# A hybrid decoder layer: one bank per part of the sample bias table, later stores of the states, and other places for three loads in sample attention

## The reference, cut to what matters

```
z = rmsnorm(x) @ w_in                      # 7 groups of 512 columns: retention q,k,v,gate; attention q,k,v
retention: o = (q k^T * decay) v + q S     # 8 heads of 64; samples start from the given state S
           S_new = S * g^C + k^T v         # state_ret_sample is an output: (8, 8, 64, 64)
attention: p = softmax(q k^T + bias[distance]);  o = p v
           # samples see a cache of 2048 keys per sequence through the dilated patterns
mix = [retention, attention] @ w_out;  x = x + rmsnorm(mix);  x = x + rmsnorm(swiglu(x))
```

## Time and profile before

| | us |
|---|---|
| median of 3 runs (1657.44 to 1664.04) | 1659.31 |
| the profiled execution | 1659.42 |
| its span, first to last instruction | 1657.9 |
| TensorE busy, share of the span | 1553.1 (94%) |
| VectorE / ScalarE / GpSimd busy | 614.4 / 410.9 / 384.4 |
| mean granted TensorE clock | 0.977 of full |
| retention ends / prompt attention ends / sample attention ends | 447 / 606 / 725.7 |

### The profile page before, as it was taken

How to read it: one execution, slowest core, us unless ns; L and a number is a source line. 1 busy time by engine, 2 the same in 40 slices (tenths; PEclk the granted TensorE clock), 3 DMA queues, 4 the chain that set the end, 5 groups by cost and what they waited for, 6 DMA issues and landing times.

```text
span 1657.9 us, 23040 instructions
## 1 busy us (share of the span) xinstructions
PE 1553.1 (94%) x9294; PEld 1345.7 (81%) x9294; DVE 614.4 (37%) x985; ACT 410.9 (25%) x728; POOL 384.4 (23%) x459
## 2 busy tenths in 40 slices
PE   7999999989888878979999999999999999999994
PEld 6788888878555556758899999999999999999983
DVE  2334110107766644524542323232323333333364
ACT  4410122112145533523432121111112111111121
POOL 3255300014322222004562121121212121111111
PEclk9999999989899999979999999999999999999997
DMA  5423434128444039923446543545535365453445
GB/s 201 126 77 127 133 127 163 47 100 293 138 140 153 14 141 412 414 84 115 124 127 191 141 148 106 169 126 152 153 113 159 108 154 138 129 159 107 132 119 165
DMA packets 120290, 245.59 MB, mean 148 GB/s; under 512 B 20652, under 2 KB 82364, under 8 KB 115045
## 3 DMA queue, kind: packets, MB, share of 16 engines
q1 hardware_dynamic: 111400, 157.15, 30.1%
q0 software_dynamic: 6976, 71.32, 14.5%
q10 hardware_dynamic: 1824, 15.83, 2.3%
HBM read 214.08 MB, written 106.21 MB: 193 GB/s over the span
## 4 chain that ended last, share of the span: by engine, by line
PE 47%; POOL 3%; issue 2%; DVE 2%; DMA 1%; ACT 0%; POOLq 0%; ACTq 0%; DVEq 0%
PE y_ps L2181 31%; PE x_ps L2195 8%; PE m_ps L2195 4%; PE d_ps L2195 4%; POOL xm L1655 1%; POOL h_lo L1667 1%; PE y_ps L1785 1%; DMA own<-x_mid_scratch 1%; DVE y L1750 1%; DVE acc L2112 0%; DVE acc L2116 0%; POOL stat L1648 0%; POOL stat L1657 0%; POOL stat L1991 0%; DVE acc L2100 0%
## 5 line engine op out<-in xcount | busy, mean ns | idle before, releaser
L2181 PE MATMUL y_ps<-h_hi,gu_hi 128*128 128x384 f32 (+1 forms) x1056 | 346.1, 328 | 0.0
L2181 PE MATMUL y_ps<-h_hi,gu_lo 128*128 128x384 f32 (+1 forms) x1056 | 345.8, 327 | 0.0
L2181 PE MATMUL y_ps<-h_lo,gu_hi 128*128 128x384 f32 (+1 forms) x1056 | 345.7, 327 | 0.0
L1959 POOL TENSOR_TENSOR f<-silu,f 128x384 fp32r<-128x384 f32 (+1 forms) x66 | 60.4, 915 | 605.0 <-ACT f L2021 417.6
L2181 PEld LDWEIGHTS y_ps<-h_hi,gu_hi 128*128 128x128 f32 x1056 | 198.4, 188 | 2.0
L2181 PEld LDWEIGHTS y_ps<-h_lo,gu_hi 128*128 128x128 f32 x1056 | 198.4, 188 | 1.9
L2181 PEld LDWEIGHTS y_ps<-h_hi,gu_lo 128*128 128x128 f32 x1056 | 198.4, 188 | 0.0
L508 PE MATMUL z_ps<-w_hi,h_hi 128*128 128x512 f32 x488 | 190.7, 391 | 4.3 <-POOL h_lo L336 4.3
L508 PE MATMUL z_ps<-w_lo,h_hi 128*128 128x512 f32 x488 | 190.0, 389 | 0.0
L2092 DVE TENSOR_TENSOR silu<-silu,y_ps 128x384 f32<-128x384 f32 (+1 forms) x66 | 35.1, 532 | 361.2 <-ACT silu L2018 355.5
L508 PE MATMUL z_ps<-w_hi,h_lo 128*128 128x512 f32 x432 | 168.2, 389 | 0.0
(11 more groups left out here) (251 smaller groups left out, 2218.3 us busy)
## 6 DMA issues: line engine op xcount, KB each, us to landing
ks_sample<-cache_k_win POOLq DMA_DIRECT2D x60, 544.0 KB, 6.5
vs_sample<-cache_v_win POOLq DMA_DIRECT2D x60, 544.0 KB, 7.8
raw<-w_gu SPq DMA_DIRECT2D x84, 256.0 KB, 6.6
K<-cache_k_win SPq DMA_DIRECT2D x8, 2048.0 KB
w_raw<-w_in SPq DMA_DIRECT2D x14, 1024.0 KB
z_scratch<-z_out SPq DMA_DIRECT2D x56, 256.0 KB, 2.0
raw<-w_down SPq DMA_DIRECT2D x22, 512.0 KB, 5.7
zr<-z_scratch SPq DMA_DIRECT2D x8, 1024.0 KB, 11.0
```

The lines of the kernel that those rows point to most:

```text
L1959: low = pool.tensor_tensor(f_lo[cut], f_t[:, 0:n_p], f_hi[cut].bitcast(F32), ALU.subtract)
L2181: mm = pe.matmul(bank[u % 2][:, 0:n], w[s][:, k, h, :], x[:, k, c:c + n], start=(k, m) == (0, 0), stop=(k, m) == (KT - 1, 2))
```

## The change

The table's three parts go to three PSUM banks: `table_ps` and the two banks of `qk_ps`. The products of parts 1 and 2 no longer wait for a copy (they wait once for `qkT_ready`, the last copy out of `qk_ps`), and their copies run on ScalarE behind its last square. The two stores of the sample states leave retention's SP program and stand in prompt attention's, after the values of pairs 0 and 1 and ahead of the sample keys; `sout_ready` and `S_out` are handed over. In sample attention `EARLY_KEYS` is 7 in place of 6, the rows and turned rows of output tiles 0 and 1 are loaded behind keys 7, and their x rows behind the second half of the weights.

```diff
-    def build_samples(self, dve, n):
-        dve.wait_ge(self.bias_done, n + 1)
+    def build_samples(self, eng, copy, n, bank):
+        eng.wait_ge(self.bias_done, n + 1)
         w = min(512, self.KEYS - 512 * n)
-        dve.tensor_copy(self.bias_s[:, 512 * n:512 * n + w], self.ps[:, 0:w]).then_inc(self.bias_ready, 1)
+        copy(self.bias_s[:, 512 * n:512 * n + w], bank[:, 0:w]).then_inc(self.bias_ready, 1)
...
-    def sample_products(self, pe, n):
+    def sample_products(self, pe, n, bank):
...
-        else:
-            pe.wait_ge(self.bias_ready, n)
...
-            mm = pe.matmul(self.ps[:, 0:w], self.rel_t[0:k, g].rearrange("n p c r t -> n (p c r t)"),
+            mm = pe.matmul(bank[:, 0:w], self.rel_t[0:k, g].rearrange("n p c r t -> n (p c r t)"),
...
+        table_ps = (tables.ps, *(bank.rearrange("c p n -> c (p n)") for bank in qk_ps))
...
                 store(SAMPLE)
-                sp.wait_ge(sout_ready, 8)
-                for par in range(2):
-                    sp.dma_start(state_s.rearrange("b (p r) d e -> r d b p e", r=2)[par],
-                                 S_out[HD * par:HD * par + HD]).then_inc(state_stored, 16)
                 tables.finish(sp)
...
                 square(SAMPLE)
+                for n in (1, 2):
+                    tables.build_samples(act, act.copy, n, table_ps[n])
...
-                tables.build_samples(dve, 0)
+                tables.build_samples(dve, dve.tensor_copy, 0, table_ps[0])
...
                 decode_state(3)
-                for n in (1, 2):
-                    tables.build_samples(dve, n)
...
-                tables.sample_products(pe, 0)
+                tables.sample_products(pe, 0, table_ps[0])
...
+                pe.wait_ge(qkT_ready, TT)
                 for n in (1, 2):
-                    tables.sample_products(pe, n)
+                    tables.sample_products(pe, n, table_ps[n])
...
                 load_values(0)
                 load_values(1)
+                sp.wait_ge(sout_ready, 2 * NPAIR)
+                for par in range(2):
+                    sp.dma_start(state_s.rearrange("b (p r) d e -> r d b p e", r=2)[par],
+                                 S_out[HD * par:HD * par + HD]).then_inc(retained[2], 16)
                 ahead(sp)
...
-    RING, GROUPS, EARLY_KEYS = 4, 3, 6
+    RING, GROUPS, EARLY_KEYS = 4, 3, 7
...
                 for b in range(2, DEC_B):
-                    if b in (4, 5):
-                        out.load_rows(sp, b - 4)
-                        out.load_turned(sp, b - 4)
-                        out.load_x(sp, b - 4)
                     sp.wait_ge(T_done, key_at(b - 2, STILES - 1) + 1)
                     load_keys(sp, A, z, K, K_landed, b)
+                for t in range(2):
+                    out.load_rows(sp, t)
+                    out.load_turned(sp, t)
                 sp.wait_ge(T_done, key_at(DEC_B - 2, STILES - 1) + 1)
                 out.load_weights(sp, 1, w_b)
+                for t in range(2):
+                    out.load_x(sp, t)
```

More of the change, by code:

```diff
@@ L618, in sample_products, with retention @@
             pe.wait_ge(self.rel_t_ready, 6)
-        else:
-            pe.wait_ge(self.bias_ready, n)
         for g in range(3):
             k = self.rows(g)
-            mm = pe.matmul(self.ps[:, 0:w], self.rel_t[0:k, g].rearrange("n p c r t -> n (p c r t)"),
+            mm = pe.matmul(bank[:, 0:w], self.rel_t[0:k, g].rearrange("n p c r t -> n (p c r t)"),
                            self.dist_s[0:k, g, 512 * n:512 * n + w], start=(g == 0), stop=(g == 2))
         mm.then_inc(self.bias_done, 1)
-def retention(nc, A, z, mix, ident, ret, state_p, state_s, tab, bias_p, bias_s, kept_on, stored, ahead):
+def retention(nc, A, z, mix, ident, ret, state_p, tab, bias_p, bias_s, kept_on, stored, sout_ready, ahead):
     with ExitStack() as ctx:
@@ L655, in retention @@
          mean_ready, oc_ready, sq_ready, square_sum_ready, var_ready, rstd_ready, on_ready, mix_ready, cleared, qd_ready,
-         kd_ready, vm_ready, sout_ready) = map(
+         kd_ready, vm_ready) = map(
             sem, ("state_landed", "qk_turned", "qkT_ready", "inner_done", "inT_ready", "update_done", "S_ready", "last_ready",
                   "o_done", "sum_ready", "mean_ready", "oc_ready", "sq_ready", "square_sum_ready", "var_ready", "rstd_ready",
-                  "on_ready", "mix_ready", "cleared", "qd_ready", "kd_ready", "vm_ready", "sout_ready"))
+                  "on_ready", "mix_ready", "cleared", "qd_ready", "kd_ready", "vm_ready"))
         *mix_stored, state_stored = stored
@@ L968, in __call__, with prompt_attention @@
         return self.nc.alloc_sbuf_tensor_at(name, shape, dtype, offset=here)
-def prompt_attention(nc, A, z, mix_t, bias, ident, q_n, k_n, qk_landed, clear, ahead, second_keys, spare, retained):
+def prompt_attention(nc, A, z, mix_t, bias, ident, q_n, k_n, qk_landed, clear, ahead, second_keys, spare, retained, state_s, S_out, sout_ready):
     UNITS, LAST = NPAIR * PT, NPAIR * PT - 1
@@ L2280, in hymba_layer @@
                                                              ("S_last", [128, NPAIR, HD]))]
+        sout_ready = nc.alloc_semaphore("sout_ready")
         retained = [nc.alloc_semaphore(n) for n in ("mix_stored0", "mix_stored1", "state_stored")]
-        retention(nc, A, z, mix, ident, ret, A["state_p"][0, 0], A["state_s"][0], tab, bias_p, bias_s, kept_on, retained,
+        retention(nc, A, z, mix, ident, ret, A["state_p"][0, 0], tab, bias_p, bias_s, kept_on, retained, sout_ready,
                   lambda sp: load_pair(sp, z, q_n, k_n, qk_landed, 0))
@@ L2300, in hymba_layer @@
                          lambda sp: load_keys(sp, A, z, K, K_landed, 1),
-                         Region(nc, spare_from, spare_to), retained)
+                         Region(nc, spare_from, spare_to), retained, A["state_s"][0], kept_on[1], sout_ready)
         with_2_3.close()
```

## The result

The changed kernel takes 1649.94 us, the median of 7 executions (1647.18 to 1654.17), against 1664.04 for the kernel before in the same comparison (7 executions, 1657.44 to 1667.54). The ratio is 0.9919 with an interval of 0.9903 to 0.9935: faster by some 13.5 us. The profiled execution took 1647.18, its span is 1645.6, and its mean granted clock is 0.981. Against the profiled execution of before (1659.42) that is 12.2 us. The difference of the medians is 14.1.

A forecast was written before the change was run, and what follows sets the result against it. It saw a one-bank ping-pong ending retention, then a clock fall, and a wait for keys in sample attention. Terms 5.6 + 3.6 + 6.0 + 1.0 = 16.2 us, off 1659.4, gave 1643.2 (1637 to 1652).

The forecast's parts named there:

- the clock's fall (1646.8): Rival at the retention boundary: a 2.0 us TensorE wait still lowers the clock, losing 3.6 us; chance 0.25.
- transfers (1647.7): Rival in sample attention: transfers bound it, moved loads give 2.5 us and a seventh tile none; chance 0.17.
- both (1651.3): Rival combining the clock's fall at the boundary with transfers bounding sample attention, 1651.3 us; chance 0.03.
- The barrier: Sign of being wrong at retention's end: the barrier comes later than 442.5.
- wait for K in a later cycle: Sign of being wrong in sample attention: TensorE waits on K<-z_scratch in later cycles; no wait over 1 us was expected.
- Boundary, 5.6: Retention's end: three banks remove the ping-pong, VectorE's last S_out becomes the end, 446.99 to 441.41, 5.6 us off.
- State stores in prompt attention, 0: Stores moved behind the v_n loads on SP's queue: cost taken as 0, other end 2.3 us.
- the slower rival: Prompt attention: state stores crawl and delay the second pair's k_n; gain gone if they add 21.5 us; chance 0.02.
- The clock, 3.6: Prompt attention's first work runs at full instead of half clock after a shorter TensorE wait: 3.6 us, ends 0 and 3.6.
- I take it that the clock stays: Step at the boundary: TensorE's 2.0 us wait is nearest to a 2.53 us one that kept clock 1.00.
- Moved loads, 6.0: Sample attention: output loads moved from ahead of keys 4 and 5 end the wait for keys; 6.0 us, ends 2.5 and 6.0.
- EARLY_KEYS, 1.0: Sample attention: a seventh key tile fits TensorE's wait for the exponential; 1.0 us taken, bounds 0 and 3.4.

The follow-up runs named there:

- the run that filled the wait: Kernel before plus four unread products while TensorE waits for the table bank in retention, ping-pong left as it was; ratio 0.9981.
- rows last: Changed kernel with rows and turned rows of output tiles 0 and 1 moved behind the second half of the weights; measured once, 1649.33 us.
- tail filled: Changed kernel with three unread products in TensorE's 3.09 us wait for the last exponential of sample attention; ratio 0.9916 to the kernel before.
- both: Changed kernel with rows behind the last weights and TensorE's waits filled at sample attention's end and in the out-projection; ratio 0.9905 to the kernel before.
- retention's part: Kernel before with the three banks and the moved state stores together, sample attention as before; ratio 0.9959.
- the late weights: Changed kernel with the first half of the output weights loaded behind keys 7, the second half waiting for it; ratio 0.9924 to the kernel before.

## Why the prediction was right, and where a step was not

It gave 1643.2 (1637 to 1652), forecast faster, and the change is faster, inside the range, by 13.5 us where the sum had 16.2. Of the 6.7 us between 1643.2 and the measured 1649.94, 4.6 come from the start: the sum was taken from 1659.4, and the kernel before has its median at 1664.04 in this comparison. The time by itself doesn't single out the forecast. It lies nearer to the rivals with the clock's fall (1646.8), with transfers (1647.7) and with both (1651.3), and each of these had a part in what happened.

Two of the signs that the prediction named for being wrong did come. The barrier stands at 444.7 and not before 442.5, but only since S_out ends 3.0 later, in code that the change leaves as it was; the block ends 0.28 behind it. And TensorE does wait for K in a later cycle, 1.75 us, over the 1 that was allowed. The terms:

**Boundary, 5.6: the amount is right (5.86 to 0.28), the cause is not complete.** The prediction gave the three banks the whole and the moved stores 0, with "What is late next is the chain of S_out on VectorE". The stores are late next: their issue of 2.87 us waits for S_out. Before, it ran beside the ping-pong and so looked free. The banks alone give 2.3, the stores' move 3.3. The step that failed is that the stores' issue was priced where it arrives and not where it leaves, though their being gone from the block was written down in the same paragraph.

**State stores in prompt attention, 0: right.** They take SP 5.23 us to issue and land after 7.5 in place of 6.4. k_n of the second pair is issued at 458.04, lands 16.6 later at 474.6, and is turned at 477.95: 3.3 of lead are left where 0.1 was worked out. The bound of 21.5 that the slower rival needed was far off.

```profile
477.95 1.07 PE L1173 MATMUL T_ps<-ident,k_n 128*128 128x128 f32 x8
```
```profile
state_s<-S_out SPq DMA_DIRECT2D x2, 512.0 KB, 7.5
...
k_n<-z_scratch SPq DMA_DIRECT2D x1, 512.0 KB, 16.6
```

**The clock, 3.6: the mechanism is shown by the run that filled the wait, the size was 2.4.** The first 16 transposes gained as worked out (1.09 and 1.17, against 1.97 for the first eight before). The step that failed is "I take it that the clock stays": it stays for 6 us and then falls for 3.4 us in prompt attention's thin first work, so the score product of 384 columns takes 1.52, near the 1.65 of before and not 0.92. The forecast and its first rival (the clock falls all the same) each had a part. Nor is the 2.4 there in each execution. Of the eight profiles with the moved boundary, five have 119.1 to 119.2 us in prompt attention, and three (rows last, tail filled, both) 121.5 to 122.2, as in the kernel before (121.5). In these the first transposes take 1.97 again, as in the stretches of the first of them:

```profile
446.90:449.80 2.90, 2.74 (x13) 2.75 (x14) 1.38 (x2) 0.00 (x0) 1.49 (x4) 0.50 0.58 166
453.20:460.00 6.80, 6.24 (x24) 2.88 (x24) 3.86 (x16) 3.02 (x10) 2.38 (x4) 0.50 0.83 246
```

What decides between the two was not found; TensorE's wait ahead of the first transposes is 2.18 or 2.19 us in all eight.

**Moved loads, 6.0: the amount is right (5.9 alone), the reason was not, and that is luck.** The choice of 6.0 over 2.5 rested on x's "3.2 us, 164 GB/s", from which the megabyte was given 6.4 us in SP's queue. The step that failed is that reading: as the packets show, keys 4 were already moving in those 3.2 us. The page DMA: Bandwidth & Descriptors of the Trainium skill (Queues, rings and completion order) has each DMA engine take turns between the queues that have work. The prediction drew from it that the queue's own time counts; no run here shows that. The wait for keys 4 of the run in which x alone was moved fell by 2.8, more than x's bytes explain, but the block's sum went nearly by the bytes. What the runs show in place of the reason: both megabytes came out of the same transfers. 2.1 MB at 410 GB/s are 5.1 us, where the lower end of 2.5 had counted only one of them, and the clock of 0.82 in the cycle of the wait is a likely source of the rest.

**EARLY_KEYS, 1.0: 0.2.** The step that failed is "Only the lead that the removed 2.1 MB leaves can be spent", taken for worth a microsecond. The cycles do gain 1.2 together, but at 417 GB/s and a share of 1.0 they leave no lead, and the last keys then come late; there the rival of the transfers was right. What the seventh tile brings besides is a wait for keys 7 in the last cycle, 0.6 to 1.75 us long in five of the six profiles that have it together with the moved loads, and in the profile of the change a clock of 0.86 behind it.

The sum as measured is 5.6 + 2.4 + 5.9 + 0.2 = 14.1, which the table of the first section confirms with 14.0. The comparisons of whole executions agree: retention's part, the moved loads and EARLY_KEYS alone multiply to 0.9959 x 0.9962 x 0.9999 = 0.9920, against 0.9919 for the change.

## What to carry to other kernels

When a wait at the end of a block is taken away, list what each of the other engines still has to issue there after the same event: a store that ran beside the wait is the next bound, and its move is part of the gain and not a cost. Where a loop's transfers run at a share of 1.0 and an engine waits for them, a load moved out of it gave back about its bytes at the measured rate here, and work saved on an engine gave next to nothing. A load moved out from a place where nobody waits leaves the transfers idle instead (the 0.75 of the late weights). Don't read the difference of two landings as the time of the later load: look at which packets ran in between. A clock gained by filling or shortening one wait can be lost at the next thin place, so count it only up to there.

## What the runs showed of the hardware that was not expected

- **The clock falls in retention, too, in twelve of the fourteen profiles.** In the profile after the stretch 390 to 404 reads 0.76, in that of before 1.00, with VectorE busy for 13.31 us there. The two rows:

```profile
390.00:404.00 14.00, 11.95 (x89) 11.45 (x89) 10.73 (x21) 2.33 (x4) 6.84 (x5) 0.76 0.89 264
```
```profile
390.00:404.00 14.00, 11.99 (x118) 11.40 (x117) 13.31 (x26) 3.88 (x8) 8.32 (x6) 1.00 0.85 250
```

  That is code the change does not touch. S_out ends at 441.4 or 441.6 in two profiles (before and EARLY_KEYS alone) and at 443.5 to 448.2 in the other twelve. The two without the late S_out are the two without this fall. The profile of before is one of them (1659.4 against medians of 1664 to 1667), and the difference of two single profiles can be off by up to 6.8 us for this alone.
- **A wait of 2.53 us is not safe.** It was followed by a granted clock of 1.00 in one kernel and 0.50 in another, and one of 2.2 us was followed by either.
- **Issuing two stores in 256-byte runs blocks SP's queue for 2.85 us or 5.23 us,** 2.85 to 2.88 at retention's end (six profiles) and 5.08 to 5.36 right behind the loads of values (eight). That it is the loads in front which make the difference was not tested.
